# Layer 1 of a two-layer diffusion block: gate and up products of 19 hidden tiles by seven quarter products instead of eight

## The reference, cut to what matters

```python
def swiglu(h, w1, w3, w2):
    return (jax.nn.silu(h @ w1) * (h @ w3)) @ w2
...
        x = x + g2x * swiglu(modulate(rms_norm(x, norm2_g[l]), sh2x, sc2x), ffn_w1[l], ffn_w3[l], ffn_w2[l])
...
    return rms_norm(x, final_g)
```

## Time and profile before

| | us |
|---|---|
| median of three runs | 1588.76 |
| lowest and highest | 1587.2, 1589.04 |
| span of the profiled execution | 1586.6 |
| TensorE busy in the whole span | 1549.4 |

### The profile page before, as it was taken

How to read it: one execution, slowest core, us unless ns; L and a number is a source line. 1 busy time by engine, 2 the same in 40 slices (tenths; PEclk the granted TensorE clock), 3 DMA queues, 4 the chain that set the end, 5 groups by cost and what they waited for, 6 DMA issues and landing times.

```text
span 1586.6 us, 25329 instructions
## 1 busy us (share of the span) xinstructions
PE 1549.4 (98%) x10779; PEld 1288.8 (81%) x10779; DVE 790.0 (50%) x1286; ACT 550.0 (35%) x725; POOL 539.6 (34%) x243
## 2 busy tenths in 40 slices
PE   6999999899999999999999999999999999999998
PEld 3888864578888888888888889855479998998997
DVE  5898877577565643433234343666533221221324
ACT  5744335463322212221122244255544322222233
POOL 0040046313233223232323223356643444444442
PEclk9999999999999999999999999999999999999999
DMA  9532100062333333334333122200022222223223
GB/s 375 212 120 67 55 27 1 3 226 80 120 116 124 133 119 121 133 124 142 133 128 112 66 80 67 67 14 1 1 71 90 94 94 93 93 94 106 94 94 107
DMA packets 44607, 158.55 MB, mean 100 GB/s; under 512 B 4784, under 2 KB 8240, under 8 KB 42960
## 3 DMA queue, kind: packets, MB, share of 16 engines
q1 hardware_dynamic: 44064, 156.74, 28.3%
q0 software_dynamic: 432, 0.20, 0.1%
HBM read 154.95 MB, written 2.10 MB: 99 GB/s over the span
## 4 chain that ended last, share of the span: by engine, by line
PE 75%; DVE 3%; ACT 1%; issue 1%; POOL 1%; DVEq 0%; POOLq 0%
PE psum L1859 67%; PE psum L2108 2%; PE psum L1936 1%; PE psum L2076 1%; DVE osb L1389 1%; PE psum L2007 1%; PE psum L1904 1%; DVE mx L1285 1%; POOL acc L624 1%; PE psum L2124 0%; PE psum L2093 0%; PE psum L2082 0%; PE psum L2078 0%; PE psum L2080 0%; PE psum L2032 0%
## 5 line engine op out<-in xcount | busy, mean ns | idle before, releaser
L1859 PE MATMUL psum<-act,whi 128*128 128x258 f32 (+2 forms) x3968 | 783.4, 318 | 0.0
L651 POOL TENSOR_TENSOR wlo<-raw,whi 128x1024 fp32r<-128x1024 f32 (+1 forms) x162 | 392.0, 2420 | 790.0 <-ACT whi L685 790.0
L1859 PEld LDWEIGHTS psum<-act,whi 128*128 128x128 f32 x3968 | 587.7, 189 | 56.1 <-issue 2.3
L1859 PE MATMUL psum<-act,wlo 128*128 128x512 f32 (+1 forms) x1984 | 472.1, 316 | 0.0
L1859 PEld LDWEIGHTS psum<-act,wlo 128*128 128x128 f32 x1984 | 309.1, 189 | 26.7
L685 ACT ACTIVATE whi<-raw 128x1024 fp32r<-128x1024 f32 (+1 forms) x180 | 187.1, 1040 | 334.3 <-DMA raw<-weights_dram 334.3
L1180 DVE SCALAR_TENSOR_TENSOR tmps<-psum,rs 128x256 f32<-128x256 f32 (+1 forms) x176 | 78.2, 486 | 350.5 <-PE psum L1859 347.0
L1132 DVE SCALAR_TENSOR_TENSOR product<-adr,cb 128x1024 f32<-128x1024 f32 x128 | 177.6, 1420 | 6.3 <-DMA adr<-adat_dram 3.3
L1628 DVE SCALAR_TENSOR_TENSOR xT<-psum,mod,xT 128x512 f32<-128x512 f32 x93 | 58.3, 655 | 223.3 <-PE psum L1859 223.3
L1859 PE MATMUL psum<-gh,whi 128*128 128x512 f32 x507 | 152.5, 357 | 0.0
L1859 PE MATMUL psum<-gh,wlo 128*128 128x512 f32 x507 | 152.4, 358 | 0.0
(11 more groups left out here) (210 smaller groups left out, 1310.7 us busy)
## 6 DMA issues: line engine op xcount, KB each, us to landing
raw<-weights_dram SPq DMA_DIRECT2D x180, 512.0 KB, 3.5
adr<-adat_dram SPq DMA_DIRECT2D x80, 512.0 KB, 4.6
ada_w<-ada_dram SPq DMA_DIRECT2D x8, 1024.0 KB, 13.1
xT<-x_in_dram SPq DMA_DIRECT2D x3, 1024.0 KB, 16.8
xT<-x_in_dram SPq DMA_DIRECT2D x2, 1536.0 KB, 8.2
cb<-crow_dram SPq DMA_DIRECT2D x2, 1024.0 KB, 9.7
out_dram<-fin SPq DMA_DIRECT2D x8, 256.0 KB, 2.3
stage<-weights_dram SPq DMA_DIRECT2D x1, 512.0 KB, 8.2
```

The source lines that it names most:

```text
L651: nc.gpsimd.tensor_tensor(wlo[:, s, 0:w], raw[:, s, 0:w], whi[:, s, 0:w].bitcast(F32), ALU.subtract).then_inc(sem("s_lo"), 1)
L1859: last = MM(out_[:, o:o + t1 - t0], w_, a_[:, t0:t1], start=k == order[0] and j == 0, stop=k == order[-1] and j == 2)
```

## The change

Three hidden tiles (`PLAIN`) stay as they were. For the other 19, called units, gate and up tile together are seen as the two block rows of a product with two halves of the contraction (512 each) and two halves of the tokens (256 each). Such a 2 x 2 product of blocks takes eight quarter products; Strassen's method in Winograd's form takes seven, of sums and differences of the blocks. A quarter product is 4 pieces x 3 terms = 12 matmuls of 256 columns, so a unit has 84 of these, where the two blocks of a tile had 96 of 256 or 258 columns.

- The token side (`forms`): the seven forms B11, B21, B22, T1 to T4 are made once, during the plain blocks, from tokens that are already normalised and modulated (`token_scaled`, `token_input`, `forms_summed`), and split into `fhi` and `flo` (1792 columns in each of 4 pieces).
- The weight side, for each unit: VectorE makes four sums of 512 columns (`weight_sum`: S1, S3, S2, S4), ScalarE rounds seven pieces of 512 columns (`piece_high`), GpSimd makes six low parts (`piece_low`) and VectorE the seventh (`last_piece_low`).
- The results: ScalarE copies three partial results of 256 columns out of PSUM (`first_product`, `first_sum`, `seventh_product`), VectorE adds three more to them (`quarter11`, `quarter22`, `quarter21`), and ScalarE takes the silu in two halves (`gate_first`, `gate_second`). Then come the product of gate and up (`hidden`, 512 columns) and its high and low part, as before.
- TensorE's order: product 1 of a unit, then products 4 and 3 of the unit before it, then 6, 7, 5, 2. Products 1, 6, 5 and 3 add up in one bank, and what is in it is copied out before the next is added: 6 waits for `first_product`, 5 for `first_sum`, and 3 for `quarter22`.
- The groups of layer 1 are of 5, 5, 6 and 6 hidden tiles. After a group's last unit, its products 4 and 3 run behind the first two pieces of the first w2 block.
- All weight buffers become double (high parts) or triple (raw), in units of pairs of blocks (`PAIRS`, 35 of them: 19 units and 16 pairs of w2 blocks).

The core of the diff; helpers that only name buffers and semaphores are left out:

```diff
-GROUPS = [(0, 8), (8, 7), (15, 7)]
+GROUPS = [[(0, 8), (8, 7), (15, 7)], [(0, 5), (5, 5), (10, 6), (16, 6)]]
+PLAIN = 3
...
+HI_ORDER = ["A11", "S3", "S1", "S2", "A12", "A22", "S4"]
...
+PRODUCT = {1: ("A11", "B11"), 2: ("A12", "B21"), 3: ("S4", "B22"), 4: ("A22", "T4"), 5: ("S1", "T1"), 6: ("S2", "T2"),
+           7: ("S3", "T3")}
...
+            def pair_low(j):
+                if PAIRS[j]["kind"] == "unit":
+                    for x in HI_ORDER[:-1]:
+                        piece_low(j, x)
...
+            forms_low(2)
+            forms_low(3)
+            for j in range(len(PAIRS)):
+                pair_low(j)
...
+            def pair_free(j):
+
+                if j == 1:
+                    act.wait_ge(sem("s_acc"), N1)
+                if j >= 2:
+                    before = PAIRS[j - 2]
+                    if before["kind"] == "unit":
+                        act.wait_ge(*done(before["n"], 2))
+                    else:
+                        act.wait_ge(sem("f_acc"), before["b"] + 2)
...
+                for j, p in enumerate(PAIRS):
+                    pending = PAIRS[j - 1] if j >= 1 and PAIRS[j - 1]["kind"] == "unit" else None
+                    unit = p["kind"] == "unit"
+                    if pending:
+                        gate_first(pending["n"])
+                    pair_high(j + 1, 0)
+                    if unit:
+                        first_product(p["n"])
+                    pair_high(j + 1, 1)
+                    if pending:
+                        gate_second(pending["n"])
+                    pair_high(j + 1, 2)
+                    if unit:
+                        first_sum(p["n"])
+                    if pending:
+                        hidden_high(pending)
+                    if unit:
+                        seventh_product(p["n"])
+                    pair_high(j + 1, 3)
...
+                if n == N1 - 1:
+                    for part in range(4):
+                        pair_high(0, part)
...
+                for j, p in enumerate(PAIRS):
+                    pending = PAIRS[j - 1] if j >= 1 and PAIRS[j - 1]["kind"] == "unit" else None
+                    if pending:
+                        quarter11(pending["n"])
+                    for x in ("S1", "S3", "S2"):
+                        weight_sum(j + 1, x)
+                    if pending:
+                        quarter21(pending["n"])
+                    weight_sum(j + 1, "S4")
+                    if pending:
+                        hidden(pending["n"])
+                        hidden_low(pending)
...
+                    last_piece_low(j + 1)
+                    if p["kind"] == "unit":
+                        quarter22(p["n"])
...
+            def product(n, j, x):
+
+                wx, fx = PRODUCT[x]
+                if x == 4:
+                    pe.wait_ge(*copied(n, 7))
+                if x == 3:
+                    pe.wait_ge(*quarter(n, "c22"))
+                if x == 6:
+                    pe.wait_ge(*copied(n, 1))
+                if x == 5:
+                    pe.wait_ge(*copied(n, 6))
...
+                pe.wait_ge(*pair_high_done(j, HI_ORDER.index(wx)))
+                if wx == "S4":
+                    pe.wait_ge(*last_low_done(n))
+                else:
+                    pe.wait_ge(*pair_low_done(j, HI_ORDER.index(wx)))
```

More of the change, by code:

```diff
@@ L114, with pairs_of_weights, weight_of, high_before @@
     FIRST.setdefault((_b["kind"], _b["layer"]), _n)
+N1 = FIRST[("w1", 1)] + 2 * PLAIN
+NW2 = len(GROUPS[1]) * KT
+KH = KT // 2
+HN = NX // 2
+def pairs_of_weights():
+    out = []
+    unit = 0
+    for g, (h0, nh) in enumerate(GROUPS[1]):
+        for h in range(max(h0, PLAIN), h0 + nh):
+            out.append(dict(kind="unit", g=g, h=h, n=unit, i=h - h0, first=h == max(h0, PLAIN), last=h == h0 + nh - 1))
+            unit += 1
+        for m in range(0, KT, 2):
+            out.append(dict(kind="w2", g=g, m=m, b=KT * g + m, nk=nh))
+    return out
+PAIRS = pairs_of_weights()
+S_OF = {"A11": None, "A12": None, "S2": 1, "S3": None, "S1": 0, "A22": None, "S4": 2}
+HI_PLACE = {"A11": 0, "A12": 1, "S2": 2, "S3": 3, "S1": 4, "A22": 5, "S4": 6}
+HI_ORDER = ["A11", "S3", "S1", "S2", "A12", "A22", "S4"]
+FORM = {"B11": 0, "B21": 1, "B22": 2, "T1": 3, "T2": 4, "T3": 5, "T4": 6}
+PRODUCT = {1: ("A11", "B11"), 2: ("A12", "B21"), 3: ("S4", "B22"), 4: ("A22", "T4"), 5: ("S1", "T1"), 6: ("S2", "T2"),
+           7: ("S3", "T3")}
+def weight_of(kind, layer, **at):
+    return next(n for n, b in enumerate(BLOCKS) if b["kind"] == kind and b["layer"] == layer
+                and all(b[k] == v for k, v in at.items()))
+def high_before(j):
+    return sum(7 if p["kind"] == "unit" else 2 for p in PAIRS[:j])
+def products_in_order():
+    out = []
+    for j, p in enumerate(PAIRS):
+        before = PAIRS[j - 1] if j >= 1 and PAIRS[j - 1]["kind"] == "unit" else None
+        late = [(before["n"], 4), (before["n"], 3)] if before else []
+        if p["kind"] == "unit":
+            out += [(p["n"], 1)] + late + [(p["n"], x) for x in (6, 7, 5, 2)]
+        else:
+            out += late
+    return {product: i for i, product in enumerate(out)}
+PRODUCT_AT = products_in_order()
+def low_before(j):
+    return sum(6 if p["kind"] == "unit" else 2 for p in PAIRS[:j])
 def attention_units(layer):
@@ new lines, in first_product, with first_sum, seventh_product @@
+            def first_product(n):
+                act.wait_ge(*done(n, 1))
+                A(staged[n % 2][:, S1C, :], unit_bank(n, 1), ACT.Copy).then_inc(sem("f_a"), 1)
+            def first_sum(n):
+                act.wait_ge(*done(n, 6))
+                A(staged[n % 2][:, UC, :], unit_bank(n, 6), ACT.Copy).then_inc(sem("f_a"), 1)
+            def seventh_product(n):
+                act.wait_ge(*done(n, 7))
+                A(staged[n % 2][:, C7, :], unit_bank(n, 7), ACT.Copy).then_inc(sem("f_a"), 1)
@@ L1012, in _ @@
+            for n, b in enumerate(BLOCKS[:N1]):
                 kind, L = b["kind"], b["layer"]
@@ new lines, in forms_low, with weight_sum @@
+            def forms_low(k):
+                dve.wait_ge(sem("f_fhi"), k + 1)
+                TT(flo[:, k, :, :], forms[:, 7 * k:7 * k + 7, :], fhi[:, k, :, :].bitcast(F32), ALU.subtract) \
+                    .then_inc(sem("f_loD"), 1)
+            def weight_sum(j, x):
+                if j >= len(PAIRS) or PAIRS[j]["kind"] != "unit":
+                    return
+                n = PAIRS[j]["n"]
+                if x == "S1":
+                    for w in range(2):
+                        dve.wait_ge(*raw_loaded(j, w))
+                    if j >= 2 and PAIRS[j - 2]["kind"] == "unit":
+                        dve.wait_ge(*done(PAIRS[j - 2]["n"], 2))
+                    a_, b_ = raw_piece(j, "A21"), raw_piece(j, "A22")
+                if x == "S3":
+                    a_, b_ = raw_piece(j, "A11"), raw_piece(j, "A21")
+                if x == "S2":
+                    dve.wait_ge(sem("f_s"), 4 * n + 1)
+                    a_, b_ = wsum[j % 2][0][:, :], raw_piece(j, "A11")
+                if x == "S4":
+                    dve.wait_ge(sem("f_s"), 4 * n + 3)
+                    if n >= 2:
+                        dve.wait_ge(*done(n - 2, 3))
+                    a_, b_ = raw_piece(j, "A12"), wsum[j % 2][1][:, :]
+                TT(weight_piece(j, x), a_, b_, ALU.add if x == "S1" else ALU.subtract).then_inc(sem("f_s"), 1)
```

422 lines of the change are left out of this document (369 added, 53 removed).

## The result

The changed kernel takes 1605.81 us (median of four runs, 1604.66 to 1608.31) against 1588.9 before: a ratio of 1.0109, 95% interval 1.0095 to 1.0123. The profiled span is 1603.2 us, 16.6 above the one before.

A forecast was written before the change was run, and what follows sets the result against it. TensorE's instruction stream bounds the kernel before; after the change, VectorE and GpSimd excluding each other and the engines' order do. +1.4 (three groups) + 17.6 (start) = +19.0 us on 1586.6: span 1605.6, time 1607.8, range 1578 to 1622.

The forecast's parts named there:

- The lock: VectorE with two SBUF inputs and GpSimd alternate whole instructions: 0.55 us per VectorE operation, 1.15 per GpSimd operation.
- The floor of 10.75: Middle unit: seven VectorE and six GpSimd operations under the lock need at least 10.75 us, above TensorE's 9.53.
- the walk: VectorE's steps of a middle unit laid out from quarter22 to quarter22: 11.3 us, or 12.4 if last_piece_low loses its race.
- The clock: Start: pauses could lower TensorE's clock; three products at half speed would add 4 us, left for the range.
- A matmul's distance: TensorE in a unit: 0.1134 us per matmul, 84 in 9.53 us; at the other bound 0.120, 10.08 us.
- Rival A: Whole kernel: VectorE and GpSimd hardly meet, TensorE stays the bound; 1566 us, or 1576 at 0.120 a matmul; chance 0.22.
- First unit of a group: Product 6 waits 0.64 us for ScalarE's copy, product 5 for first_sum: 10.6 us for five products needing 6.8.
- End of a group: Products 4 and 3 add 2.7 us; w2 then waits 2.2 or 1.9 us for the last hidden tile.
- The groups: Groups beyond the first: 58.4 and 69.4 us against 57.6 and 69.1; +1.4 us for the three together.
- The start: First group: TensorE waits 1.5, 10.5, 5.5 and 2.4 us around the first unit; 40.6 against 23.0 us, +17.6.
- B: Milder slowdown: periods at the floor of 10.75 us, no VectorE lag at the start; 1596 us; chance 0.20.
- C: Slower still: middle periods of 12.4 us, +12 us; 1620 us; chance 0.15.

The follow-up runs named there:

- experiment 1: Changed kernel with GpSimd's low parts of the units' weights replaced by memsets to zero: 1583.79 us, ratio 0.9969 to the kernel before.
- experiment 3: Changed kernel with two low parts (S1, S2) moved from GpSimd to VectorE: 1596.41 us, ratio 1.0038 to the kernel before.
- experiment 11: Changed kernel with the seventh low part (S4) moved from VectorE to GpSimd: 1604.73 us, ratio 1.0108 to the kernel before.
- experiment 10: Changed kernel with only ScalarE's order changed, as in experiment 5: 1599.46 us, ratio 1.0076 to the kernel before.
- experiment 5: On top of experiment 3, ScalarE copies products 1 and 6 earlier in first units and rounds the hidden tile before the second w2 block: 1586.09 us.
- experiment 6: On top of experiment 5, four plain hidden tiles instead of three: 1584.09 us, ratio 0.9971 to the kernel before.
- experiment 7: Changed kernel with the forms' four low parts replaced by memsets to zero: 1598.92 us, ratio 1.0067 to the kernel before.
- experiment 12: On experiment 6 with product 7 ahead of 6 in first units: first unit's weights prepared before the last plain block's steps; 1581.89 us.
- experiment 8: Kernel before with only layer 1's groups changed to 5, 5, 6 and 6, no quarter products: 1591.96 us, ratio 1.0019.

## Why the prediction was right, step by step

The time came out for the stated reason in the main, VectorE and GpSimd holding each other up. Where in a group TensorE would lose the time was forecast wrong, and part of the closeness of 2 us is luck.

- **The lock** (0.55 and 1.15 us for an operation): right, by experiments 1 and 3, and for GpSimd's pace by 11. The floor of 10.75 was met by 10.80 to 10.83; my 11.3 was half a microsecond too long. Up to `hidden_low` the walk is met: it ends 8.77 us after `quarter22` for 8.75. The half is ScalarE's: A12, A22 and S4 are rounded by 9.6 us where I had 10.1, since two such operations in a row take 1.14 us and not 1.26. `last_piece_low`, my uncertain place (up to 12.4), took 0.87.
- **Where TensorE loses it:** wrong. I charged every middle unit 11.3 us. The eight took 9.9 to 10.8, 8.0 us less in all, and the wait of product 6 for `first_product` that the walk has in each of them didn't appear. The first and second units took 5.7 us more than I had. That the total held isn't all luck: in experiment 10 the first units fall to 7.6 to 7.9 us and the others rise to 10.7 to 12.0, and the units of a group together take 52.9, 63.8 and 62.7 us for 53.3, 64.3 and 63.3. So ScalarE's order moved this loss about and hardly changed it. That my wrong split adds up to the right total is luck.
- **The clock:** left out of the sum. Product 5's wait in the three first units is followed by 3.4 us at half clock each time, some 16 matmuls at 0.213 us instead of 0.118, 1.5 us. Little of this counted: experiment 10 has neither these waits nor these stretches, and its groups are the 0.4 to 0.6 us shorter just given.
- **A matmul's distance.** I took 0.1134 from the earlier trace rows; in the units it is mostly 0.118, nearer to the other bound. Rival A was priced wrong: without the lock the kernel ran 1583.8, not 1566 or 1576, since a unit needs 9.9 us of TensorE and not 9.5, and the start (8.6 us) and the ends of groups (7.3 us) still wait. The Trainium skill's rule of 0.109 (TensorE: Matmul & The Clock Gate, Back-to-back issue gap) is further off.
- **First unit of a group:** product 6 waits 0.64, as worked out, and product 5 2.9, 3.0 and 2.2 for 3.2 (distances of starts less one matmul; the waits view counts 0.2 to 0.3 us less). The units were still 1.8, 1.8 and 1.0 us longer than the 10.6 forecast, by the half clock and the matmul's distance. **End of a group:** 2.1, 2.1, 1.8 and 1.8 for 2.2 and 1.9. The cause, the order of ScalarE's queue and GpSimd's residue, is borne out by experiments 5 and 10.
- **The groups:** 58.2, 69.0 and 67.9 us for 58.4, 69.4 and 69.4. That is 0.7 below the time before, where I had 1.4 above. These are distances between the groups' first products, less the w2 matmuls at 0.233.
- **The start:** the waits were 0.4, 9.4 and 4.0 us for 1.5, 10.5 and 5.5, and product 5's 2.4 didn't appear. What the waits fell short, half clock gave back in part: I had left it out of the sum, and some 33 matmuls went at 0.213 us instead of 0.118, about 3 us; 1.1 of them, in product 1, only made product 6's wait shorter. Group 0 came to 39.4 for 40.6. The cause is shown by experiments 6, 7 and 12: the forms' residues, and behind them the lock. (The forecast's own terms, 1247.5 + 6.8 + 5.5 + 2.4, end at 1262.2 and not at 1261.6.)
- **The sum:** -0.7 + 16.4 = 15.7 of the 16.6 us; 0.8 of the other 0.9 lie ahead of it all: TensorE's products behind the normalisation start at 1204.85 for 1204.07 before. Why wasn't traced.
- **Rivals B and C** were priced with 11 periods, while my own sum has 8 at 11.3. With 8 they come to about 1598 and 1617; the measured time lies between B and the forecast either way.
- **What I had not priced** is the grouping: of the 17 us, 3 are there without a single quarter product (experiment 8). In the units' sum they are part of the waits at w2.
